# The up stage of a decoder layer: eight gathered rows in every round, x1 loaded at the front

## What is computed

```python
def token_block(args):
    xb, eb, gb = args
    act = jax.nn.gelu(jnp.einsum('pd,phkd->phk', xb, expert_down[eb]).astype(f32), approximate=False)
    return jnp.einsum('phk,phkd->pd', (gb * act).astype(x.dtype), expert_up[eb])
...
x = layer_norm(ALPHA * x + ffn, ln2_gain[layer], ln2_bias[layer])
```

## Time and profile before

| | |
|---|---|
| median of three runs | 4245.97 us (4236.12 to 4256.16) |
| the profiled execution, its time | 4250.72 us |
| the profiled execution, its span | 4249.0 us |
| mean granted TensorE clock | 0.966 |
| busy over the span | PE 94%, PEld 84%, DVE 60%, POOL 39%, ACT 32% |
| the up stage | about 3110 us to the end |

### The profile page before, as it was taken

One profiled execution on the slowest core, in us unless ns is written; L12 is line 12 of the kernel. 1 busy time (PEld: TensorE's weight loads), 2 busy tenths in 40 slices (PEclk: granted clock), 3 DMA queues, 4 the chain that ended last, 5 costly groups with the idle time before them and its releaser, 6 DMA issues. The chain is left out here.

```text
span 4249.0 us, 59296 instructions
## 1 busy us (share of the span) xinstructions
PE 3982.7 (94%) x21744; PEld 3589.1 (84%) x21744; DVE 2557.7 (60%) x5137; ACT 1368.9 (32%) x2139; POOL 1667.6 (39%) x1134
## 2 busy tenths in 40 slices
PE   8999998978888898999999999999989999999998
PEld 7888886878888778999999999999977777777886
DVE  1135113555555453148688878876558777777888
ACT  2134223642222211113744626537321212222221
POOL 0000013514444000005367565575535555555654
PEclk8999998989999999999999999999999999999999
DMA  3223344641223422234489697798977878787885
GB/s 106 99 99 123 123 128 119 157 115 40 77 77 100 159 98 84 79 127 116 105 265 287 195 317 233 239 333 249 324 264 274 287 257 278 271 283 269 305 286 201
DMA packets 390356, 801.61 MB, mean 189 GB/s; under 512 B 64944, under 2 KB 203696, under 8 KB 389168
## 3 DMA queue, kind: packets, MB, share of 16 engines
q1 hardware_dynamic: 279600, 530.95, 37.4%
q0 software_dynamic: 110592, 268.62, 20.9%
HBM read 623.15 MB, written 154.27 MB: 183 GB/s over the span
## 5 line engine op out<-in xcount | busy, mean ns | idle before, releaser
L2032 PE MATMUL r_psd<-x1h,r_dh 128*128 128x384 f32 x2048 | 700.1, 342 | 7.5 <-DVE r_dl L1830 7.4
L2032 PE MATMUL r_psd<-x1h,r_dl 128*128 128x384 f32 x2048 | 687.5, 336 | 0.0
L2032 PE MATMUL r_psd<-x1l,r_dh 128*128 128x384 f32 x2048 | 687.5, 336 | 0.0
L2276 PE MATMUL e_psy<-e_uh,e_Ch 128*128 128x512 f32 x1536 | 610.2, 397 | 57.8 <-DVE e_Cl L2199 57.8
L2276 PE MATMUL e_psy<-e_ul,e_Ch 128*128 128x512 f32 x1536 | 607.6, 396 | 0.0
L2276 PE MATMUL e_psy<-e_uh,e_Cl 128*128 128x512 f32 x1536 | 606.4, 395 | 0.0
L1805 POOL DMA_INDIRECT W<-r_put,r_place x256 | 426.2, 1665 | 391.7 <-DVEq L1979 304.4
L2222 DVE SCALAR_TENSOR_TENSOR e_y<-e_rows,coef,e_y 128x1024 f32<-128x1024 f32 x254 | 361.2, 1422 | 171.3 <-DMA e_rows<-in_up,ids 163.6
L1796 POOL DMA_INDIRECT r_rows<-in_down_rows,ids x256 | 267.0, 1043 | 352.7 <-DVE coef L1847 235.6
L2276 PEld LDWEIGHTS e_psy<-e_uh,e_Ch 128*128 128x128 f32 x1536 | 294.5, 192 | 125.8 <-issue 48.5
L2032 PEld LDWEIGHTS r_psd<-x1h,r_dh 128*128 128x128 f32 x2048 | 387.9, 189 | 8.2 <-DVE r_dl L1830 8.2
(11 more groups left out here) (339 smaller groups left out, 7474.8 us busy)
## 6 DMA issues: line engine op xcount, KB each, us to landing
hand<-in_down SPq DMA_DIRECT2D x128, 512.0 KB
hand<-in_up SPq DMA_DIRECT2D x128, 512.0 KB
act<-r_act SPq DMA_DIRECT2D x128, 384.0 KB
e_W<-W SPq DMA_DIRECT2D x128, 384.0 KB
W<-r_W SPq DMA_DIRECT2D x32, 1024.0 KB
p_wraw<-in_w_in SPq DMA_DIRECT2D x58, 512.0 KB, 4.4
hT<-p_out SPq DMA_DIRECT2D x58, 512.0 KB, 2.9
hand<-act SPq DMA_DIRECT2D x64, 384.0 KB
```

The costliest lines, as they stand in the source:

```text
L2032: ins = nc.tensor.matmul(psd[n][:, h, 0:HD], a[c % DEEP][:, k, :], b[:, k, h * HD:(h + 1) * HD], start=(k == 0 and m == 0), stop=(k == KD ...
L2276: ins = nc.tensor.matmul(bank[:], a[s][:, t * P:(t + 1) * P], v[s][:, h * HALF:(h + 1) * HALF], start=(q == 0 and m == 0), stop=(q == G - ...
```

## The change

`per_round` becomes eight in all 32 rounds. The first eight gathers are issued behind the weighting of chunks 4 to 7 instead of behind that of chunk 7 and later ones. SP loads all eight blocks of x1 straight into `y`, in one go behind the load of chunk 3. VectorE waits for all of them before its first addition, scales the two gathered blocks by ALPHA, and folds ALPHA * y into the first addition of each dense half bank. `add_x`, its tile and its loads go. In the last round two rows stand behind each of the first four additions, and the norm passes begin at the fifth. Since all rounds are alike, VectorE's and SP's code for the middle rounds becomes a Fori loop over pairs of rounds (VectorE) or chunks (SP), with addresses and wait values in registers.

```diff
-    per_round = [0, 10] + [8] * (NR - 4) + [12, 0]
-    for n in range(NU - sum(per_round)):
-        per_round[3 + 2 * n] += 1
-    x_round = [3 + 3 * t for t in range(TT)]
+    per_round = [NU // NR] * NR
...
+            def loads(i):
+                for n in range(2):
+                    sp.wait_ge(sem("C_lo"), START + 2 * i + (n + 1))
+                    load(2 * i + (n + 2), n)
+
+            loads(0)
+            for t in range(TT):
+                sp.dma_start(y[:, t, :], g.x1[t * P:(t + 1) * P, :]).then_inc(sem("ld_y"), 16)
+            with sp.Fori(1, NCH // 2 - 1) as i:
+                loads(i)
...
             for c in range(2 * G):
                 weigh(c)
+                if c >= G:
+                    for k in range(NGU // G * (c - G), NGU // G * (c - G + 1)):
+                        gather(k)
...
-                if r == 0:
-                    ins = nc.vector.tensor_copy(o, bank)
+                if first:
+                    ins = nc.vector.scalar_tensor_tensor(o, o, ALPHA, bank, ALU.mult, ALU.add)
...
+            dve.wait_ge(sem("ld_y"), START + 16 * TT)
+            for t in GATHERED:
+                nc.vector.tensor_scalar(y[:, t, :], y[:, t, :], ALPHA, None, ALU.mult).then_inc(sem("y_init"), 1)
+            dve.wait_ge(sem("y_init"), START + NG2)
+            rounds(0, 0, first_up[0], per_round[0], prepared=1, first=True)
+            rounds(1, 1, first_up[1], per_round[1], prepared=2)
+            with dve.Fori(1, NR // 2 - 1) as i:
+                for par in range(2):
+                    rounds(2 * i + par, par, first_up[2 + par], per_round[2], i=i, prepared=2 * i + (1 + par))
+            rounds(NR - 2, 0, first_up[NR - 2], per_round[NR - 2], prepared=NR - 1)
             for b in range(BR):
-                add(NR - 1, b)
-                if 1 <= b <= 4:
-                    finish(dve, b - 1)
...
+                add(NR - 1, 1, b)
+                if b < 4:
+                    for k in range(2 * b, 2 * b + 2):
+                        accumulate(first_up[NR - 1] + k)
                 else:
-                    done = NG2 + b // 2 if b % 2 == 1 else None
+                    if b > 4:
+                        finish(dve, b - 5)
+                    if b < BR - 1:
+                        for h in range(2):
+                            stats_of(dve, b - 4, h)
+                        centre(dve, b - 4)
```

More of the change, by code:

```diff
@@ L2044 @@
     "y_add rstd stats aggr var centred final ld_A0 ld_A1 ld_u0 ld_u1 C_lo ld_y ld_ln st_out "
-    "y_mm u_hi weighted C_hi power x_added final_last acc", "ld_r0 ld_r1 ld_r2 ld_r3 ld_r4 ld_r5 ld_r6 ld_r7")
+    "y_mm u_hi weighted C_hi power y_init final_last acc", "ld_r0 ld_r1 ld_r2 ld_r3 ld_r4 ld_r5 ld_r6 ld_r7")
 def stage_up(nc, g):
@@ L2056, in stage_up @@
     NU = NG2 * P
-    per_round = [0, 10] + [8] * (NR - 4) + [12, 0]
-    for n in range(NU - sum(per_round)):
-        per_round[3 + 2 * n] += 1
-    x_round = [3 + 3 * t for t in range(TT)]
+    per_round = [NU // NR] * NR
     assert sum(per_round) == NU
     first_up = [sum(per_round[:r]) for r in range(NR)]
+    PER_PASS = 2 * per_round[2]
     with ExitStack() as ctx:
@@ L2067, in stage_up @@
         sem = g.sem.__getitem__
-        y, x = sb("e_y", [P, TT, D]), sb("e_x", [P, D])
+        y = sb("e_y", [P, TT, D])
         uraw = g.hand[0:2]
@@ L2116, in load @@
                 for d, s, name in ((araw[n], g.act, "A"), (Wt[n][:], g.W, "A"), (uraw[n][:], g.up, "u")):
-                    sp.dma_start(d, s[c]).then_inc(sem(f"ld_{name}{n}"), 16)
+                    sp.dma_start(d, s[bass.ds(c, 1)].rearrange("o p k -> (o p) k")).then_inc(sem(f"ld_{name}{n}"), 16)
             sp.dma_start(Wt[0][:], g.W[0]).then_inc(sem("ld_A0"), 16)
@@ L2176, in _ @@
                 weigh(c)
+                if c >= G:
+                    for k in range(NGU // G * (c - G), NGU // G * (c - G + 1)):
+                        gather(k)
             for r in range(NR):
                 for q in range(G):
-                    if r == 0:
-                        for k in range(NGU // G * q, NGU // G * (q + 1)):
-                            gather(k)
                     if r + 2 < NR:
                         weigh(G * (r + 2) + q)
-                    for k in range(first_up[r] + per_round[r] * q // G, first_up[r] + per_round[r] * (q + 1) // G):
+                    each = per_round[r] // G
+                    for k in range(first_up[r] + each * q, first_up[r] + each * (q + 1)):
                         if k + NGU < NU:
@@ L2199, in low, with add @@
                 nc.vector.tensor_tensor(Cl[s][:], araw[n], Ch[s][:].bitcast(F32), ALU.subtract).then_inc(sem("C_lo"), 1)
-            def add(r, b):
+            def add(r, par, b, first=False):
                 dve.wait_ge(sem("y_mm"), START + BR * r + (b + 1))
                 o = y[:, DENSE[b // 2], b % 2 * HALF:(b % 2 + 1) * HALF]
-                bank = psy[(BR * r + b) % NB][:]
-                if r == 0:
-                    ins = nc.vector.tensor_copy(o, bank)
+                bank = psy[(BR * par + b) % NB][:]
+                if first:
+                    ins = nc.vector.scalar_tensor_tensor(o, o, ALPHA, bank, ALU.mult, ALU.add)
                 else:
@@ L2210, in add, with accumulate @@
                 ins.then_inc(sem("y_add"), 1)
-            def accumulate(k):
+            def accumulate(k, i=None):
                 u, n, e = k % NGU, k % NG2, k // NG2
[L2215 to L2220, removed]
-                else:
-                    ins = nc.vector.scalar_tensor_tensor(o, rows[u][:], scale, o, ALU.mult, ALU.add)
-                ins.then_inc(sem("acc"), 1)
@@ L2225, in add_x @@
[L2225 to L2234, removed]
+                turn = 0 if i is None else i - 1
@@ new lines, in accumulate @@
+                dve.wait_ge(sem(f"ld_r{u}"), 16 * (k // NGU + 1) + 16 * (PER_PASS // NGU) * turn)
+                if k > 0:
+                    dve.wait_ge(sem("acc"), START + k + PER_PASS * turn - 1)
+                o = y[:, GATHERED[n], :]
+                if i is None:
+                    scale = g.coef[:, n, e:e + 1]
+                else:
+                    scale = g.coef[:, n, bass.ds(PER_PASS // NG2 * i + (e - PER_PASS // NG2), 1)]
+                nc.vector.scalar_tensor_tensor(o, rows[u][:], scale, o, ALU.mult, ALU.add).then_inc(sem("acc"), 1)
@@ L2236, in _, with rounds @@
+            def rounds(r, par, at, count, i=None, prepared=None, first=False):
+                done = 0
+                for b in range(BR):
+                    add(r, par, b, first)
+                    while done < count * (b + 1) // BR:
+                        accumulate(at + done, i)
+                        done += 1
+                    if prepared is not None and b % 2 == 1 and b // 2 < G:
+                        low(prepared, 1 - par, b // 2)
             for q in range(G):
                 low(0, 0, q)
[L2238 to L2248, removed]
@@ L2249, in _ @@
-            for b in range(BR):
-                add(NR - 1, b)
-                if 1 <= b <= 4:
-                    finish(dve, b - 1)
[L2253 to L2258, removed]
-                else:
-                    done = NG2 + b // 2 if b % 2 == 1 else None
+            dve.wait_ge(sem("ld_y"), START + 16 * TT)
+            for t in GATHERED:
+                nc.vector.tensor_scalar(y[:, t, :], y[:, t, :], ALPHA, None, ALU.mult).then_inc(sem("y_init"), 1)
@@ L2261, in _ @@
                 if b == BR - 2:
                     stats_of(dve, TT - 1, 0)
[L2263 to L2266, removed]
+            stats_of(dve, TT - 1, 1)
+            centre(dve, TT - 1)
             finish(dve, TT - 1)
```

## The result

The changed kernel took 4200.49 us (median of four runs, 4198.87 to 4205.8), the kernel before 4248.42 us on the same chips; the ratio is 0.9899, 95% interval 0.9883 to 0.9915. The forecast was 4205 us and faster. The profiled execution took 4201.67 us, with a span of 4199.9.

A forecast was written before the change was run, and what follows sets the result against it. TensorE was taken to bound the up stage, VectorE's queue with its gathers setting the stalls. 3110.0 + 1011.8 + 7.5 + 17 + 2 = 4148.3, plus 57.3 gives 4205.6 us of span; forecast 4205 us, range 4192 to 4226.

The forecast's parts named there:

- Rounds 3 to 23, 67.0 us back: Up stage: without ninth rows and x1 additions each round takes 32.64 us, so 67.0 us come back.
- echo: Rounds after the front: the margin does not return in one round; 2 us charged, bounds 0 and 12.
- Front, 17 us: Stage start: round 1 starts at 3165.4, not 3148.5, so 17 us are lost, bounds 13 and 23.
- the transfer of x1: Front, SP's queue: 4.19 MB ahead of chunk 4 take 13 us; chunk 4 lands at about 3137, 9 us late.
- the gather: Front: from the gather's issue behind the weighting of chunk 4 to VectorE's row 0, 6.9 us.
- From first to fourth product: Front, VectorE's products for round 1: the fourth follows the first by 18 us, between 14 and 24.
- Registers and loops, 0: VectorE's and SP's Fori loops: register steps and loop ends cost 0 us.
- Last round, T + 57.3: From the last round's first matmul, T, to the end: 57.3 us, before 51.75; tail 5.6 us longer, bounds 3 and 9.
- Sum: Whole kernel: T at 4148.3 plus 57.3 gives a span of 4205.6 us, 43.4 less than before.
- the first (stalls stay): Up stage: eight rows are no cure, stalls in each second round cost 55 us; 4260, no gain; chance 0.07.
- the third (the loop costs): VectorE's loop: stalls per pair of rounds or register steps make the kernel slower, about 4275 us; chance 0.04.
- the second, a dearer front: Rounds 1 to 6: gathers, x1 and chunks fight, 15 to 30 us more, 4220 to 4235; chance 0.12.

The follow-up runs named there:

- e3: Kernel before with the ninth row of nine-row rounds placed behind the last bank on VectorE; 4214.65 us, ratio 0.9914.
- e6: Kernel before with only the gathers of nine-row rounds split 3, 2, 2, 2 over the slots, not 2, 2, 2, 3; 4210.64 us, ratio 0.9915.
- e4: Changed kernel with VectorE's and SP's loops written out, constant addresses and wait values; 4198.36 us, ratio 0.9877.
- e9: e5 with the four extra rows of round 30 moved to rounds 23, 25, 27 and 29, fourteen nine-row rounds; 4185.67 us, ratio 0.9863.
- e5: Kernel before with the ninth row last in its round and gathers split 3, 2, 2, 2; 4181.42 us, ratio 0.9854; again 4187.81 us, 0.9873.
- e1: Kernel before with eight rows in every round and the change's front gathers and last round, x1 as before, no loops; 4190.44 us, ratio 0.9861.
- e2: Kernel before with x1 loaded at the front and folded into the first additions, table of rows as before, no loops; 4245.07 us, ratio 0.9989.
- e7: Changed kernel with the eight rows of round 0 placed behind banks 8 to 11; 4194.05 us, ratio 0.9874.

## Why the prediction was right, point by point

*Rounds 3 to 23, 67.0 us back.* Right in size, by 29 rounds at 32.64 us, and better than my 2 us for an echo: there was none. The reason for the stalls was half right. That one more row in VectorE's queue, ahead of the fourth product, uses the margin up is shown by e3 and e6, but it is about half of it. I named the row's gather too, but did not see that the ninth row shifts the next round's gathers behind a weighting that hangs on that round's own product. The wait of 1.83 us before round 23, which I read as a margin that had not yet come back, fits this: it follows an eight-row round behind a nine-row one, it stands in e3 (3.03 us) and is gone in e6. An even table removes both causes, which is why the forecast did not suffer: here the number had luck that the reason had not earned.

*Front, 17 us.* 12.8 measured, just under my lower bound of 13: rounds 0 and 1 took 85.6 us, where 72.8 in the earlier trace rows. Two terms were mis-sized. The first is the transfer of x1, "I take 13". x1 did follow chunk 3, as I had it, but from 3120.60 to 3130.83 took 10.2 us, at 411 GB/s where I had reckoned with 271 to 338; so chunk 4 was read at 3134.09 and not at 3137, 5.1 us later than before counted from the stage's first matmul. The second is the gather: 3139.07 - 3134.84 = 4.2 us where I had taken 6.9, from a stretch in which the queues moved 340 GB/s, against 232 here. From first to fourth product it was 19.3 us where I had 18. One wait came out longer: TensorE stood at bank 10 of round 0 until 3143.01 and not 3136, for an addition that stands behind the first row and the first product; it still lies inside the wait for round 1.

The Trainium skill (DMA: Bandwidth & Descriptors, HWDGE ordering) says that descriptors are consumed in ring order on each DMA engine. The trace agrees: chunk 4, issued from 3122.42 while x1 was under way, is read only after x1 has landed at 3130.83, and from 3120.60 to 3130.80 the queues moved just x1's bytes.

*Registers and loops, 0.* Shown by e4. The Trainium skill (Runtime: NRT & Kernel Launch, Instruction fetch mechanics) warns of a stall where a taken branch leads outside the two pages held. None appeared: the loop end takes 40 and 56 ns, 14 times, and rounds 2 to 30 lose nothing. A pass has only 124 recorded instructions of VectorE, though, and whether its branch ever leads outside what is held is not shown.

*Last round, T + 57.3.* 57.1 measured. The rows in it cost 5.4 us over before, as reckoned (5.6), and e9 shows the other side: without rows there and in round 30 no more than eight, it is 47.7.

*Sum.* 4205.6 us of span, and it was 4199.9; of the 5.7 the front is 4.2 and the echo 2, the tail 0.2, and the stage began 0.6 later. Of the rivals, the first (stalls stay) and the third (the loop costs) did not happen; the second, a dearer front, went the other way. What the forecast lacked is a rival that turned out best: the gain needed neither eight rows nor x1 at the front, and one half of the change eats some 8 us of what the other gives.

## What to carry to other kernels

When a stall comes in every second round, look one round back on every in-order queue: an extra item costs its own time where it stands, and it also shifts the items behind it into later slots, which may hang on work of the same round. Before evening out a whole schedule, try where the extra item stands and how a division is rounded; here three lines (e5) gave 65 us of the stage where the full rewrite gave 50. A bulk load moved to the front delays what is queued behind it, and more so what hangs on that: here x1 made chunk 4 5.1 us later, and round 1 8.6 us later than in e1 (51.0 against 42.4 us behind round 0).

## What was unexpected of the hardware

The 4.19 MB of x1 in one backlog, with two chunks ahead and two behind, moved at 411 GB/s (395 in e2 from 3105.7 to 3122.5), more than the 338 of the best stretch that I had read before. VectorE's sequencer steps at the loop end took 40 to 80 ns each and showed nowhere between the instructions. And the start of this stage lay up to 10 us apart between runs (3102.4 in e2, 3112.4 in e7), though no edit touches an earlier stage: more than several of the effects measured here. Single times can't tell those apart; the stage's own length can, down to the 2 us by which it differs itself.
